# Tokens in order of their residue modulo four in the second attention layer of a 256-token decoder

## The chip, the cores and the metric

The kernel is one launch on one NeuronCore of a Trainium2 chip. The metric is the device time of that launch in microseconds (us), the median of several runs. TensorE (PE in the rows) multiplies matrices into PSUM, VectorE (DVE), ScalarE (ACT) and GpSimd (POOL) work element by element, and SyncE (SP) issues most of the DMAs. Every engine works through its own instructions in the order in which they are written; semaphores order the engines among each other.

## What is computed

The input is one sequence of 256 tokens of width 1024, in float32. Two decoder layers follow each other, each with a mixer and a SwiGLU. The first mixer (A) is stick-breaking attention with 16 heads of 64. The second (B) is an attention in three groups, each with its own queries, keys and values of 16 heads, whose outputs are mixed by their softmax denominators. Cut to what matters here:

```python
DILATED_GROUPS = ((128, 1), (512, 4), (2048, 16))      # (window, dilation)

def dilated_group_attention(qb, kk, vv, rel_bias, window, dilation):
    # queries and keys of one residue class modulo the dilation
    rel = Q_BLOCK + i - m
    band = (rel >= 0) & (rel <= window // dilation)
    bias = rel_bias[relative_bucket(rel * dilation)]
    s = einsum(qb, kk) * HEAD_DIM ** -0.5 + bias
    s = jnp.where(valid, s, NEG_INF)
    lse = logsumexp(s); p = exp(s - lse[..., None])
    return einsum(p, vv), lse

def mixer_b(xn, shared_kv, w_q, w_o, rel_bias):
    ...
    wts = jax.nn.softmax(lse, axis=0)                   # over the three groups
    o = jnp.sum(wts[..., None] * o, axis=0)
    return o.reshape(b, s, D_MODEL) @ w_o

# the layer around either mixer
x = x + rms_norm(h, g[1]);  h = swiglu(rms_norm(x, g[2]), w_gate_up, w_down);  x = x + rms_norm(h, g[3])
```

The mixing over the groups makes one softmax over the keys of all three groups together. In group 0 a token sees the 128 tokens before it and itself. In groups 1 and 2 it sees only tokens whose distance is a multiple of 4 or of 16, so only tokens of its own residue modulo 4.

## The kernel before, in words

Everything is written out by hand for each engine; there is no scheduler. Tokens stand in two tiles of 128 partitions (t = 0 and 1), tokens 0 to 127 and 128 to 255.

**Weights.** They come in 138 units of up to 1 MB. SP loads a unit into one of three raw buffers (L274 to L283; it waits for `lo_made`, which frees the buffer), ScalarE copies it as the high part `w_hi` (`hi`, L430), VectorE subtracts that and writes the low part `w_lo` (`lo`, L690), and TensorE multiplies high by high, high by low and low by high in float32r (`by_x`, L1091, and `by_w`, L1097). Six cut units can stand at a time.

**Stages.** Layer A: eight pairs of heads, each projected (`project_a`) while the pair before it is attended; each pair's output is turned into `ot`, high and low part (`cut_ot`, L770). Then the output projection (`out_proj`), the update of the residual `xn`, the SwiGLU. Layer B is the same with `step_b`: while the queries, keys and values of pair p are projected, the attention of pair p - 1 is worked on between these products. A step, in TensorE's order (L1381): `scores_b`, four blocks of columns, the nine transposes of head 0, a block, the nine transposes of head 1, a block, half the values, `outputs_b`, the other half.

**Attention B before the change.** For each head and group, `scores_b` (L1334) multiplies the first query tile by 128 keys (`short`) and the second by all 256 (`long`), in plain float32. VectorE adds the bias and takes the peak (`scored`, L882), 384 and 768 columns a head; ScalarE takes the exponential (L523), VectorE divides (`normalize`, L907), TensorE transposes 9 blocks of 128x128 into banks 4 to 6 of PSUM, the same three for both heads (L1366), so that the transposes of head 1 wait (L1363) until ScalarE has copied those of head 0 (`transposed_b`, L527). `outputs_b` (L1369) multiplies the transposed weights by the values: in each group 256 query columns for the first key tile, 128 for the second.

**The bias.** One line per head of 384 values is made at the start and stored in device memory (L390). In layer B, GpSimd loads for each head a band of 128x256 from it with one DMA (`head_bias`, L401 to L412), each partition one element further along, and adds it to the mask of all three groups, 768 columns in one instruction. VectorE waits for the bias of both heads of a pair before the peaks (L893).

**The output.** SP stores four pieces of 128x512 (L342 to L346) as their updates are made.

Of the kernel before, what the change touches and what calls it, by code (L numbers as in the profile page):

```python
# [28 lines left out]
SEQ = 256  # L29
P = 128  # L30
NT = SEQ // P
KT = D // P
NH = 16
# [6 lines left out]
NG = len(GROUPS)  # L40
BUCKETS = 32
# [22 lines left out]
def shape_constants():  # L64
# [7 lines left out]
    dist = P + i[:, None] - np.arange(2 * P)[None, :]  # L72
    mask = np.zeros((P, NG, 2 * P), np.float32)
    for g, (window, dilation) in enumerate(GROUPS):
        seen = (dist >= 0) & (dist % dilation == 0) & (dist // dilation <= window // dilation)
        mask[:, g] = np.where(seen, 0.0, OUTSIDE)

    n = np.maximum(np.arange(3 * P) - (P - 1), 0)
# [8 lines left out]
def build(nc, x, norm_gains, w_qkv_a, w_o_a, g_kv, w_kv_b, w_q_b, w_o_b, rel_bias, w_gate_up, w_down,  # L87
# [7 lines left out]
    out_dram = out[0].rearrange("(t p) d -> t p d", p=P)  # L95
# [7 lines left out]
    bias_rows = nc.dram_tensor("bias_rows", [NH, 3 * P], F32, kind="Internal").ap()  # L103

    with ExitStack() as ctx:
# [8 lines left out]
        bands = bass.AP(bias_rows.tensor, bias_rows.offset, [[3 * P, NH], [1, P], [1, 2 * P]])  # L114
# [12 lines left out]
        mask_b = sb("mask_b", [P, NG, 2 * P], BF16)  # L127
# [15 lines left out]
        select_in = carve(3 * P)  # L143
        rel_in = carve(NH)
        mask_in = carve(NG * 2 * P).rearrange("p (g s) -> p g s", g=NG)
        bias_out = carve(3 * P)
# [25 lines left out]
        W0, W1 = NG * P, NG * 2 * P  # L172
        prob = [carve(W0 + W1) for _ in range(2)]
        turned = [v.rearrange("p (g n) -> p g n", g=NG) for v in prob]
        bias = carve(2 * W1).rearrange("p (b g s) -> p b g s", b=2, g=NG)
        band = carve(2 * P)
# [25 lines left out]
        w_used = sem("w_used")  # L202
        x_in = [sem(f"x_in{t}") for t in range(NT)]
# [51 lines left out]

        def hidden_at(i):

            return slice(2, 4) if i == STEPS - 1 else slice(0, 2)


# [12 lines left out]
        def _(sp):  # L273
# [58 lines left out]
            sp.dma_start(mask_in, mask).then_inc(mask_in_s, 16)  # L332
            for u in range(4):
# [8 lines left out]
            for t in range(NT):  # L342
                for half in range(2):
                    sp.wait_ge(x_made, 6 * NT + 2 * t + half + 1)
                    cols = slice(HALF * half, HALF * half + HALF)
                    sp.dma_start(out_dram[t][:, cols], xn[:, t, cols]).then_inc(out_stored, 16)  # L346
            sp.wait_ge(out_stored, 32 * NT)
# [3 lines left out]
        def _(pool):  # L351
# [38 lines left out]
            pool.dma_start(bias_rows, bias_out[0:NH, :]).then_inc(bias_stored, 16)  # L390
            pool.wait_ge(bias_stored, 16)
# [9 lines left out]
            def head_bias(b, h):  # L401
# [4 lines left out]
                pool.dma_start(band, bands[ds(h, 1)].rearrange("h t s -> (h t) s")).then_inc(band_in, 16)  # L406
# [1108 lines left out]
```

## Time and profile before

| | |
|---|---|
| median of 3 runs | 793.88 us (793.18 to 794.0) |
| profiled execution | 794.14 us, span 792.5 us |
| TensorE busy | 782.9 us, 99% of the span |
| VectorE, ScalarE, GpSimd busy | 502.9, 378.2 and 61.7 us |
| granted clock of TensorE | full, 1.00 |
| DMA | 135.45 MB, mean 171 GB/s |

The matmul durations of the profile overlap, since the next product starts before the last has drained; what a matmul costs the path is read from the chain of work that ended last, which gives each only the time that it adds. Busy time of the other engines costs nothing while TensorE finds its inputs ready. A plain float32 matmul has two records in the trace, a transpose has one.

### The profile page before, as it was taken

The page shows a single profiled execution, that of the slowest core. Times are in us where ns is not written, and L with a number is a line of the kernel's source. Part 1 is how long each engine was busy: PE and PEld are TensorE (multiplying, and loading weights), DVE is VectorE, ACT ScalarE, POOL GpSimd, SP SyncE. Part 2 cuts the span into 40 slices and gives each one's busy share as a digit, 9 for nine tenths or more (in the row PEclk, how much of TensorE's full clock was granted, in tenths as well). Part 3 has the DMA queues.
Part 4 walks back from the last instruction along what each step waited for, and adds up shares of the span by engine and source line. Part 5 has one row for each costly group of instructions (what it writes and reads, how often), then busy time and mean ns, then how long its engine had stood idle before and what let it go on. Part 6 is the DMA issues. An engine that isn't in the chain of part 4 may idle for free.

```text
span 792.5 us, 12896 instructions
## 1 busy us (share of the span) xinstructions
PE 782.9 (99%) x4789; PEld 687.8 (87%) x4789; DVE 502.9 (63%) x632; ACT 378.2 (48%) x452; POOL 61.7 (8%) x76
## 2 busy tenths in 40 slices
PE   8999999999999999999999999999999999999997
PEld 7999978888888888998999999999988888888885
DVE  6888987764555646875746647567547755455453
ACT  5665667443434334934545435445357443443331
POOL 2000001100000000330201202112002000000000
PEclk9999999999999999999999999999999999999999
DMA  7534755676556555567556465474722874555601
GB/s 225 164 114 129 241 184 179 229 252 217 178 161 206 166 186 153 136 183 197 138 156 176 122 174 163 126 205 117 258 77 69 293 258 159 181 189 189 219 16 53
DMA packets 158818, 135.45 MB, mean 171 GB/s; under 512 B 5193, under 2 KB 149185, under 8 KB 158785
## 3 DMA queue, kind: packets, MB, share of 16 engines
q1 hardware_dynamic: 157312, 130.75, 52.7%
q0 software_dynamic: 1376, 4.22, 2.5%
q8 instruction: 21, 0.34, 0.2%
q14 instruction: 13, 0.10, 0.1%
q10 hardware_dynamic: 96, 0.04, 0.0%
HBM read 133.91 MB, written 1.07 MB: 170 GB/s over the span
## 4 chain that ended last, share of the span: by engine, by line
PE 94%; DVE 2%; ACT 1%; DMA 1%; issue 1%; SPq 0%; DVEq 0%; POOLq 0%; POOL 0%; ACTq 0%
PE ps L1093 20%; PE ps L1095 19%; PE ps L1094 19%; PE ps L1099 8%; PE ps L1101 8%; PE ps L1100 8%; PE ps L1376 2%; PE ps L1366 2%; PE ps L1241 1%; PE ps L1345 1%; DVE w_lo L693 1%; PE ps L1170 1%; PE ps L1339 1%; DMA raw<-in_w_q_b 1%; PE ps L1181 1%; PE ps L1148 1%
## 5 line engine op out<-in xcount | busy, mean ns | idle before, releaser
L693 DVE TENSOR_TENSOR w_lo<-raw,w_hi 128x2048 fp32r<-128x2048 f32 (+2 forms) x144 | 277.3, 1945 | 34.0 <-ACT w_hi L434 32.3
L434 ACT ACTIVATE w_hi<-raw 128x2048 fp32r<-128x2048 f32 (+2 forms) x144 | 232.3, 1637 | 45.3 <-DMA raw<-in_w_kv_b 11.4
L1093 PE MATMUL ps<-w_hi,xt 128*128 128x512 f32 x352 | 139.5, 396 | 0.0
L1095 PE MATMUL ps<-w_hi,xt 128*128 128x512 f32 x352 | 137.3, 390 | 0.0
L1094 PE MATMUL ps<-w_lo,xt 128*128 128x512 f32 x352 | 137.1, 389 | 0.0
L575 ACT ACTIVATE work<-ps,stat 128x256 f32<-128x256 f32 x44 | 20.9, 476 | 199.1 <-PE ps L1095 199.1
L1099 PE MATMUL ps<-xt,w_hi 128*128 128x256 f32 x384 | 110.2, 287 | 0.7 <-DVE w_lo L994 0.7
L1100 PE MATMUL ps<-xt,w_hi 128*128 128x256 f32 x384 | 108.6, 283 | 0.0
L1101 PE MATMUL ps<-xt,w_lo 128*128 128x256 f32 x384 | 108.6, 283 | 0.0
L1093 PE MATMUL ps<-w_hi,ot 128*128 128x512 f32 x240 | 94.9, 395 | 0.4 <-DVE w_lo L693 0.4
L1094 PE MATMUL ps<-w_lo,ot 128*128 128x512 f32 x240 | 93.5, 390 | 0.0
L1095 PE MATMUL ps<-w_hi,ot 128*128 128x512 f32 x240 | 93.5, 390 | 0.0
L1095 PEld LDWEIGHTS ps<-w_hi,xt 128*128 128x128 f32 x352 | 66.1, 188 | 14.0
L1093 PEld LDWEIGHTS ps<-w_hi,xt 128*128 128x128 f32 x352 | 66.1, 188 | 13.6 <-issue 0.6
L1094 PEld LDWEIGHTS ps<-w_lo,xt 128*128 128x128 f32 x352 | 66.2, 188 | 12.9
L1099 PEld LDWEIGHTS ps<-xt,w_hi 128*128 128x128 f32 x384 | 73.5, 191 | 4.3 <-issue 3.0
L1100 PEld LDWEIGHTS ps<-xt,w_hi 128*128 128x128 f32 x384 | 73.5, 192 | 0.0
L1101 PEld LDWEIGHTS ps<-xt,w_lo 128*128 128x128 f32 x384 | 73.5, 192 | 0.0
L953 DVE CAST ot<-ps 128x512 fp32r<-128x512 f32 x22 | 15.2, 692 | 78.2 <-PE ps L1241 78.2
L1099 PE MATMUL ps<-xkv,w_hi 128*128 128x256 f32 x192 | 55.5, 289 | 0.0
L1093 PEld LDWEIGHTS ps<-w_hi,ot 128*128 128x128 f32 x240 | 45.1, 188 | 10.8 <-DVE w_lo L693 1.0
L1101 PE MATMUL ps<-xkv,w_lo 128*128 128x256 f32 x192 | 54.3, 283 | 0.0
(130 smaller groups left out, 1100.9 us busy)
## 6 DMA issues: line engine op xcount, KB each, us to landing
raw<-in_w_gate_up SPq DMA_DIRECT2D x88, 512.0 KB, 4.7
raw<-in_w_kv_b SPq DMA_DIRECT2D x96, 256.0 KB, 3.6
raw<-in_w_down SPq DMA_DIRECT2D x22, 1024.0 KB, 4.9
raw<-in_w_q_b SPq DMA_DIRECT2D x48, 256.0 KB, 3.7
raw<-in_w_qkv_a SPq DMA_DIRECT2D x23, 512.0 KB, 4.8
raw<-in_w_o_a SPq DMA_DIRECT2D x4, 1024.0 KB, 5.4
raw<-in_w_o_b SPq DMA_DIRECT2D x4, 1024.0 KB, 5.2
work<-in_norm_gains POOLq DMA_DIRECT2D x4, 512.0 KB, 5.2
```

What stands on the lines that cost most here:

```text
L434: act.activation(w_hi[:, s % CUT, 0:size(s)], raw[:, s % RAW, 0:size(s)], ACT.Copy).then_inc(hi_made, 1)
L575: act.activation(silu[:, t, :], bank(4 + t, 0, FC), ACT.Silu, scale=x_rs(2 * l + 1, t)).then_inc(silu_made, 1)
L693: dve.tensor_tensor(w_lo[:, c, 0:n], raw[:, s % RAW, 0:n], w_hi[:, c, 0:n].bitcast(F32), ALU.subtract).then_inc(lo_made, 1)
L953: dve.tensor_copy(ot[:, 0, k, :], src).then_inc(ht_hi, 1)
L1093: mm(out, xs[0], ws[0], start=start, stop=False)
L1094: mm(out, xs[0], ws[1], start=False, stop=False)
L1095: return mm(out, xs[1], ws[0], start=False, stop=stop)
L1099: mm(out, ws[0], xs[0], start=start, stop=False)
L1100: mm(out, ws[0], xs[1], start=False, stop=False)
L1101: return mm(out, ws[1], xs[0], start=False, stop=stop)
L1366: inst = pe.transpose(bank(4 + g, P * n, P), prob[hh][:, at_:at_ + P], eye[:, :])
L1376: inst = mm(ps[DH * hh:DH * hh + DH, at_:512 * 7 + SEQ], vb[:, kt, P * g + DH * hh:P * g + DH * hh + DH], turned[hh][:, g, cols], start=g ...
```

## The change

From the first output projection on, the tokens stand in another order: all tokens with residue 0 modulo 4 first, then 1, 2 and 3, 64 each. Tile 0 holds residues 0 and 1, tile 1 residues 2 and 3. What it takes:

- The outputs of attention A are written to `ot` in the new order (VectorE reads PSUM with a step of four values).
- `x` is loaded a second time in the new order into `xn`, by four DMAs of 64x1024 from SP, behind the mask and before the weights of the output projection. The first update of `xn` waits for them.
- In groups 1 and 2 a tile only sees itself, so a query tile has 256 + 128 + 128 = 512 score columns in either tile, one bank of PSUM. The scores of the two heads stand in banks 2 to 5, the transposes of head 0 in banks 4 and 5 and of head 1 in banks 6 and 7; the wait of head 1's transposes for the copy of head 0's goes.
- The bias lines are seven per head, by difference of residues, and are stored with two DMAs. A head's band is 2x128x256 instead of 128x256, and comes with four DMAs of 64x4x64 (runs of 64 values, 256 bytes) instead of one of 128x256. The sum with the mask, still 768 columns, is in two instructions.
- The output is stored in eight pieces of 64x512, two of them from ScalarE's queue.

```diff
@@ sync
             sp.dma_start(mask_in, mask).then_inc(mask_in_s, 16)
+            sp.wait_ge(xt_done, 4)
+            sp.wait_ge(xsq_made, NT)
+            for r in range(R):
+                sp.dma_start(xn[RUN * (r % 2):RUN * (r % 2) + RUN, r // 2, :], by_residue(x[0])[r]).then_inc(x_again, 16)
...
-                    sp.dma_start(out_dram[t][:, cols], xn[:, t, cols]).then_inc(out_stored, 16)
+                    store(sp, t, half, 0)
+                    if t == 0:
+                        store(sp, t, half, 1)
@@ gpsimd
-            pool.dma_start(bias_rows, bias_out[0:NH, :]).then_inc(bias_stored, 16)
+            pool.dma_start(bias_rows[:, R - 1:2 * R - 1, 0:2 * RUN - 1], found[:, :, 1:2 * RUN]).then_inc(bias_stored, 16)
+            pool.dma_start(bias_rows[:, 0:R - 1, 0:2 * RUN - 1], found[:, 1:R, 0:2 * RUN - 1]).then_inc(bias_stored, 16)
...
-                pool.dma_start(band, bands[ds(h, 1)].rearrange("h t s -> (h t) s")).then_inc(band_in, 16)
-                pool.wait_ge(band_in, h * 16 + 16)
+                for r in range(R):
+                    pool.dma_start(band[RUN * (r % 2):RUN * (r % 2) + RUN, r // 2, :].rearrange("p (c n) -> p c n", c=R),
+                                   bands[r][ds(h, 1)].rearrange("h m c n -> (h m) c n")).then_inc(band_in, 16)
+                pool.wait_ge(band_in, (h * 16 + 16) * R)
...
-                pool.tensor_tensor(bias[:, b], mask_b[:, :, :],
-                                   band[:, ::-1].rearrange("p (g s) -> p g s", g=1).broadcast_to([P, NG, 2 * P]),
-                                   ALU.add).then_inc(bias_made, 1)
+                pool.tensor_tensor(ends[0], ends[1], turned_band, ALU.add)
+                pool.tensor_tensor(middle[0], middle[1], turned_band[:, 0:1, 0:P].broadcast_to([P, 2, P]), ALU.add
+                                   ).then_inc(bias_made, 1)
@@ scalar
-                act.activation(turned[hh], banks(4, NG, W0), ACT.Copy).then_inc(pt_made, 1)
+                act.activation(turned[hh], ps[:, 512 * (4 + 2 * hh):512 * (6 + 2 * hh)], ACT.Copy).then_inc(pt_made, 1)
...
+            for half in range(2):
+                act.wait_ge(x_made, 8 * NT - 1 + half)
+                store(act, NT - 1, half, 1)
@@ vector
+                    if b == 0 and t == 0 and half == 0:
+                        dve.wait_ge(x_again, 16 * R)
...
-                dve.tensor_copy(ot[:, 0, k, :], src).then_inc(ot_hi, 1)
+                hi_, lo_ = (ot[:, h, ds(k, 1), :].rearrange("p o (r m) -> p (o r) m", r=R) for h in range(2))
+                dve.tensor_copy(hi_, src).then_inc(ot_hi, 1)
                 dve.wait_ge(ot_hi, n)
-                dve.tensor_tensor(ot[:, 1, k, :], src, ot[:, 0, k, :].bitcast(F32), ALU.subtract).then_inc(ot_made, 1)
+                dve.tensor_tensor(lo_, src, hi_.bitcast(F32), ALU.subtract).then_inc(ot_made, 1)
...
+                cut_ot(j * 2 + a, bank(7, 0, SEQ).rearrange("p (m r) -> p r m", r=R), j * 2 + a + 1)
@@ tensor, scores_b
-                short(0)
-                long(0)
+                one(0, 0, 0, slice(0, SEQ))
+                one(1, 0, SEQ, slice(0, SEQ))
                 pe.wait_ge(qkb_made, j * 6 + 3 * a + 3)
-                short(1)
-                short(2).then_inc(s_done, 1)
-                long(1)
-                long(2).then_inc(s_done, 1)
+                one(0, 1, SEQ, slice(0, P))
+                one(0, 2, SEQ + P, slice(0, P)).then_inc(s_done, 1)
+                one(1, 1, 0, slice(P, SEQ))
+                one(1, 2, P, slice(P, SEQ)).then_inc(s_done, 1)
@@ tensor, transpose_b
-                if hh:
-                    pe.wait_ge(pt_made, h)
-                for g in range(NG):
-                    for n, at_ in enumerate((P * g, W0 + 2 * P * g, W0 + 2 * P * g + P)):
-                        inst = pe.transpose(bank(4 + g, P * n, P), prob[hh][:, at_:at_ + P], eye[:, :])
+                for t in range(NT):
+                    for n in range(4):
+                        kind = n if t == 0 else (n + 2) % 4
+                        inst = pe.transpose(bank(4 + 2 * hh + kind // 2, SEQ * (kind % 2) + P * t, P),
+                                            prob[hh][:, WB * t + P * n:WB * t + P * n + P], eye[:, :])
@@ tensor, outputs_b
-                    for kt, cols in ((0, slice(0, SEQ)), (1, slice(SEQ, SEQ + P))):
+                    for kt in range(NT):
+                        cols = slice(0, SEQ) if g == 0 else slice(P * kt, P * kt + P)
```

How TensorE's instructions stand in a step of layer B, before. This is inside the loop over the pairs; `work` holds queries, keys, weights and values of attention B, `xkv` the input of the projections. The three pieces are the scores, the transposes of head 0 and the outputs:

```order
1205 L1339 MATMUL ps<-work 128x128 x2
1206 L1345 MATMUL ps<-work 128x256 x2
1207 L1352 REGISTER_ALU
1208 L1339 MATMUL ps<-work 128x128 x4
1209 L1345 MATMUL ps<-work 128x256 x4
...
1312 L1366 MATMUL ps<-eye,work 128x128 x9
...
1389 L1095 MATMUL ps<-w_hi,xkv 128x384
1390 L1376 MATMUL ps<-work 64x256 x2
1391 L1376 MATMUL ps<-work 64x128 x2
1392 L1376 MATMUL ps<-work 64x256 x2
1393 L1376 MATMUL ps<-work 64x128 x2
1394 L1376 MATMUL ps<-work 64x256 x2
```

The same three pieces in the changed kernel:

```order
1205 L1363 MATMUL ps<-work 128x256 x4
1206 L1371 REGISTER_ALU
1207 L1363 MATMUL ps<-work 128x128 x8
...
1310 L1384 MATMUL ps<-eye,work 128x128 x8
...
1387 L1119 MATMUL ps<-w_hi,xkv 128x384
1388 L1396 MATMUL ps<-work 64x256 x4
1389 L1396 MATMUL ps<-work 64x128 x8
```

Scores and outputs stay at twelve matmuls each for a pair, with four wide ones where there were six; each head has eight transposes instead of nine. What stands around them has not moved.

GpSimd's queue at the start of attention B, before: the bias of the first two heads, then the start of the loop.

```order
33 L406 DMA work<-bias_rows 128x256 [waits x_made]
34 L410 TENSOR_TENSOR work<-mask_b,work 128x768 [waits band_in]
35 L406 DMA work<-bias_rows 128x256 [waits bias_made]
36 L410 TENSOR_TENSOR work<-mask_b,work 128x768 [waits band_in]
37 L416 UNCONDITIONAL_BRANCH
```

The same place in the changed kernel:

```order
34 L432 DMA work<-bias_rows 64x4x64 [waits x_made]
35 L432 DMA work<-bias_rows 64x4x64 x3
36 L440 TENSOR_TENSOR work<-mask_b,work 128x2x256 [waits band_in]
37 L441 TENSOR_TENSOR work<-mask_b,work 128x256
38 L432 DMA work<-bias_rows 64x4x64 [waits bias_made]
39 L432 DMA work<-bias_rows 64x4x64 x3
```

Each head now has four DMAs and two sums where it had one and one, in the same place of the queue.

## Rows read from the trace of the kernel before

**Rows 1.** The page: busy time, and the chain that ended last by engine.
```profile
PE 782.9 (99%) x4789; PEld 687.8 (87%) x4789; DVE 502.9 (63%) x632; ACT 378.2 (48%) x452; POOL 61.7 (8%) x76
...
PE 94%; DVE 2%; ACT 1%; DMA 1%; issue 1%; SPq 0%; DVEq 0%; POOLq 0%; POOL 0%; ACTq 0%
```

**Rows 2.** Waits of TensorE over the whole span: total us, times, longest.
```profile
PE ps L1404 <- DVE rows L983: 1.3, 1, 1.3
PE ps L1366 <- ACT work L530: 1.3, 1, 1.3
```

**Rows 3.** The chain, one later step of B: start us, us that it adds.
```profile
403.72 2.10 PE ps L1376 x24
...
410.19 0.42 PE ps L1339 x4
410.61 0.43 PE ps L1345 x4
411.05 0.44 PE ps L1339 x8
411.49 0.87 PE ps L1345 x8
...
424.06 0.98 PE ps L1366 x9
```

**Rows 4.** TensorE's transposes of B as a group: busy us, mean ns, idle before.
```profile
L1366 PE MATMUL ps<-eye,work 128*128 128x128 f32 x144 | 18.4, 273 | 1.3 <-ACT work L530 1.3
```

**Rows 5.** TensorE in the first step of B: start us, us, idle before.
```profile
357.99 1.15 PE L1366 MATMUL ps<-eye,work 128*128 128x128 f32 x9
...
363.30 1.17 PE L1366 MATMUL ps<-eye,work 128*128 128x128 f32 x9 [1.30 <-ACT work L530]
```

**Rows 6.** GpSimd from the first band on, the same columns.
```profile
326.34 0.62 POOL L406 DMA_DIRECT2D work<-bias_rows  x1
331.55 1.67 POOL L410 TENSOR_TENSOR work<-mask_b,work 128x768 f32<-128x768 bf16 x1 [4.58 <-DMA work<-bias_rows]
333.51 0.57 POOL L406 DMA_DIRECT2D work<-bias_rows  x1 [0.30 <-POOL work L410]
336.75 1.65 POOL L410 TENSOR_TENSOR work<-mask_b,work 128x768 f32<-128x768 bf16 x1 [2.67 <-DMA work<-bias_rows]
...
354.17 1.66 POOL L410 TENSOR_TENSOR work<-mask_b,work 128x768 f32<-128x768 bf16 x1 [2.97 <-DMA work<-bias_rows]
...
381.50 1.66 POOL L410 TENSOR_TENSOR work<-mask_b,work 128x768 f32<-128x768 bf16 x1 [24.46 <-DVE stat L885]
```

**Rows 7.** VectorE in the first step of B.
```profile
344.65 1.75 DVE L693 TENSOR_TENSOR w_lo<-raw,w_hi 128x1536 fp32r<-128x1536 f32 x1
346.32 0.55 DVE L885 CUSTOM_DVE_ANT_1 work<-ps,work 128x384 f32<-128x384 f32 x1
...
354.13 2.44 DVE L915 TENSOR_SCALAR work<-work,stat 128x384 f32<-128x384 f32 x2
```

**Rows 8.** DMA issues: count, KB of each, median us to landing.
```profile
raw<-in_w_q_b SPq DMA_DIRECT2D x48, 256.0 KB, 3.7
...
work<-in_norm_gains POOLq DMA_DIRECT2D x4, 512.0 KB, 5.2
work<-bias_rows POOLq DMA_DIRECT2D x16, 128.0 KB, 3.5
...
out_x<-xn SPq DMA_DIRECT2D x4, 256.0 KB, 2.1
```

**Rows 9.** SP's queue between the layer A loads: start us, us.
```profile
82.78 1.32 SPq L332 DMA_DIRECT2D work<-in_mask  x1
90.53 0.38 SPq L282 DMA_DIRECT2D raw<-in_w_o_a  x1
```

**Rows 10.** VectorE at the last cut of layer A.
```profile
119.36 0.42 DVE L772 CAST ot<-ps 128x256 fp32r<-128x256 f32 x1 [1.50 <-PE ps L1183]
119.82 0.42 DVE L774 TENSOR_TENSOR ot<-ps,ot 128x256 fp32r<-128x256 f32 x1
```

More of the change, by code:

```diff
@@ L40 @@
 NG = len(GROUPS)
+R = GROUPS[1][1]
+RUN = SEQ // R
 BUCKETS = 32
@@ L70, in shape_constants @@
     square = np.stack([eye, later, strict, np.ones((P, P), np.float32)], 1)
-    dist = P + i[:, None] - np.arange(2 * P)[None, :]
-    mask = np.zeros((P, NG, 2 * P), np.float32)
-    for g, (window, dilation) in enumerate(GROUPS):
+    token = R * (np.arange(SEQ) % RUN) + np.arange(SEQ) // RUN
+    parts = []
+    for t, g, keys in ((0, 0, SEQ), (0, 1, P), (0, 2, P), (1, 0, SEQ)):
+        window, dilation = GROUPS[g]
+        dist = token[P * t:P * t + P, None] - token[None, 0:keys]
         seen = (dist >= 0) & (dist % dilation == 0) & (dist // dilation <= window // dilation)
-        mask[:, g] = np.where(seen, 0.0, OUTSIDE)
-    n = np.maximum(np.arange(3 * P) - (P - 1), 0)
+        parts.append(np.where(seen, 0.0, OUTSIDE))
+    mask = np.concatenate(parts, 1).astype(np.float32)
+    n = np.maximum((R * (np.arange(2 * RUN)[None, :] - RUN) + np.arange(R)[:, None]).reshape(-1), 0)
     exact = BUCKETS // 2
@@ L110, in sem @@
             return ctx.enter_context(nc.semaphore(name))
-        bands = bass.AP(bias_rows.tensor, bias_rows.offset, [[3 * P, NH], [1, P], [1, 2 * P]])
+        bands = [bass.AP(bias_rows.tensor, bias_rows.offset + 2 * RUN * r,
+                         [[(2 * R - 1) * 2 * RUN, NH], [1, RUN], [2 * RUN, R], [1, RUN]]) for r in range(R)]
         raw = sb("raw", [P, RAW, UNIT])
@@ L171, in build @@
         vb = carve(NT * NG * P).rearrange("p (t n) -> p t n", t=NT)
[L172 to L176, printed above, removed]
+        WB = 4 * P
+        prob = [carve(NT * WB) for _ in range(2)]
+        turned = prob
+        bias = carve(2 * (WB + SEQ)).rearrange("p (b s) -> p b s", b=2)
+        band = carve(NT * SEQ).rearrange("p (t s) -> p t s", t=NT)
         def column(first):
@@ L202, in build @@
         w_used = sem("w_used")
+        x_again = sem("x_again")
         x_in = [sem(f"x_in{t}") for t in range(NT)]
@@ L254, in arrived, with store, by_residue @@
             return 16 * sum(parts(u) for u in range(s % RAW, s + 1, RAW))
+        def store(queue, t, half, r):
+            cols = slice(HALF * half, HALF * half + HALF)
+            queue.dma_start(by_residue(out[0])[2 * t + r][:, cols], xn[RUN * r:RUN * r + RUN, t, cols]
+                            ).then_inc(out_stored, 16)
         def hidden_at(i):
             return slice(2, 4) if i == STEPS - 1 else slice(0, 2)
+        def by_residue(v):
+            return v.rearrange("(m r) d -> r m d", r=R)
         def x_block(k, t, tiles=1):
@@ L1335, in scores_b, with one @@
                 heads = [slice(DH * hh, DH * hh + DH) for hh in range(2)]
-                def short(g):
+                def one(t, g, at_, keys):
                     for hh, r in enumerate(heads):
-                        inst = mm(bank(2 + 3 * hh, P * g, P), qb[r, g, 0:P], kb[r, g, 0:P], start=True, stop=True)
-                    return inst
-                def long(g):
-                    for hh, r in enumerate(heads):
-                        at_ = 512 * (3 + 3 * hh) + SEQ * g
-                        inst = mm(ps[:, at_:at_ + SEQ], qb[r, g, P:SEQ], kb[r, g, :], start=True, stop=True)
+                        inst = mm(bank(2 + 2 * hh + t, at_, keys.stop - keys.start), qb[r, g, P * t:P * t + P],
+                                  kb[r, g, keys], start=True, stop=True, skip_group_check=True)
                     return inst
```

62 lines of the change are left out of this document (26 added, 36 removed).

## The prediction

> **What bounds the kernel now.** I read the page first: TensorE is busy for 99% of the span and 94% of the chain that ended last is its work [rows 1]. Then its waits: over the whole span it waited 1.3 us before its first instruction, 1.3 us once for a copy of ScalarE, and the other entries of the list are under a microsecond each [rows 2]. So this kernel is a string of matmuls, and a change moves its time in two ways only: by the columns that TensorE has to stream, and by an input that comes late enough to make it wait. The chain says what a matmul adds to the string. Its records there, unlike the busy times, don't overlap [rows 3]. After that I looked at who feeds layer B beside the weights: GpSimd with the bias. In later steps its sum is ready and idles 24.46 us for the buffer that VectorE frees; only in the first step is it close [rows 6, 7].
>
> **What TensorE saves, step by step.** A plain float32 matmul has two records. In the scores, 8 records of 256 columns take 0.87 us and 8 of 128 columns 0.44 us [rows 3], so a matmul of 256 columns costs 0.217 us and one of 128 costs 0.11 us.
>
> - Scores: before, 6 matmuls of 256 and 6 of 128 a pair, 6 x 0.217 + 6 x 0.11 = 1.96 us (the chain has 0.42 + 0.43 + 0.44 + 0.87 = 2.16, of which 0.2 is the start of the group, which stays). After, 4 of 256 and 8 of 128: 1.75. Saved 0.21.
> - Outputs: the same counts before and after. Before they add 2.10 us [rows 3], 1.96 and the start. Saved 0.21.
> - Transposes: 9 add 0.98 us [rows 3], 0.109 each. Two fewer a pair: saved 0.22.
>
> That is 0.64 us a pair, and with 8 pairs (the 144 transposes of the trace are 8 x 18 [rows 4]) 5.2 us.
>
> The rate of the outputs could be another after the change, where eight matmuls of 128 columns stand in a row, which before came two at a time. In the scores four of them already stand in a row, and go at the rate of their columns (the 0.44 us for 8 records). So I take no loss; it is a rival below.
>
> On the price of float32 the Trainium skill has another number: "True FP32: 4 passes through PE array" (FP8 and Floating Point Precision, section TensorE Precision Notes). The trace shows two records for such a matmul, and the 0.217 us for 256 columns. By the page's four passes at the full clock, 256 columns would take an estimated 0.43 us, the savings of scores and outputs would double, and the sum would come out 3.4 us lower than mine. The measured duration decides here.
>
> **The wait that goes.** In the first step of B the transposes of head 1 start at 363.30 us after 1.30 us of idle time, for ScalarE's copy of head 0 out of the banks that both heads share [rows 5]. After the change each head has its own banks, so this wait has no object. What is late next at this place is `norm_made` of head 1, whose two multiplications ended with those of head 0 well before (354.13 + 2.44 = 356.57 for head 0, about 1.2 us more for head 1 [rows 7]), 4 us ahead. The copies of both heads are needed by the outputs some 8 us later. I take the full 1.3 us. In no other step did TensorE wait there, since the idle time of the group is this one wait [rows 4].
>
> **What is added.**
>
> - The bias lines: one matmul of 512 columns instead of 384, 0.11 us more on the path, at the start of the kernel. The second store of the lines has 200 us of cover until the first band.
> - `x` again: 1 MB in four DMAs on SP's queue. What stands behind them are the weights of the output projection. SP's last issue before was at 82.78 us and took 1.32, the next was at 90.53, when its buffer came free [rows 9]. Four issues of 0.4 to 1.3 us end by 89.4 at the latest. So SP is ready in time, and its queue holds nothing else meanwhile. The user, the first update of `xn`, comes after the last cut of layer A, which stood at 119.82 [rows 10], 30 us later. Cost 0; with the cover gone, one landing, about 4 us (a 256 KB load lands in 3.7 [rows 8]).
> - The step of four in VectorE's read of PSUM for `ot`: two instructions of 0.42 us for each pair [rows 10]. No row shows a strided read from PSUM. Lower end 0 (the count of elements is the same), upper end twice the time, 0.9 us a pair. VectorE is busy for 63% of the span, so only the last pair, on which the output projection waits, can put it on the path: 0 to 0.9 us, and I take 0.
> - Less work for VectorE and ScalarE in B (1024 instead of 1152 columns a head in peaks, exponential, division and copy): off the path, 0.
> - The stores: the last one was 256 KB and landed in 2.1 us [rows 8]. Now two of 128 KB go from two queues at the same time. Bounds -0.5 to +0.6 us; I take 0.
>
> **The bands are the open cost.** Four DMAs of 256 runs instead of one of 128 rows, twice the bytes, for each of 16 heads. Call D the time from the first issue of a head to the last landing. Before, D was 5.2 us for head 0 (326.34 to 331.55) and 3.2 for head 1 [rows 6]. Bias of both heads was ready at 336.75 + 1.65 = 338.4, and VectorE asked for it at 346.32, behind a cut of weights [rows 7]. With two heads one after the other, the bias is ready at 326.3 + 2D + 2 x 1.8 (the sums, a little more in two parts) + 0.6 between = 330.5 + 2D. It is on time up to D = 7.9. Queued behind the waiting VectorE are the peaks, two cuts of weights and the division; the transposes of head 0, at 357.99, had 1.4 us of room behind the division's end at 356.57, and that division took 2.44 us because a GpSimd sum ran from 354.17 to 355.83, which will now come later. With shorter peaks that gives some 2 us of room, so TensorE begins to wait at about D = 9.
>
> For D I have: one issue of 128 rows takes 0.57 us and lands in 3.5 (median) [rows 6, 8]. Lower end: four issues at 0.57, the last landing 3.5 to 5.2 after its own, D = 5.2 to 6.9. If an issue goes with its runs (256 instead of 128), it takes 1.1 us and D is 7 to 8.6. Upper end: everything goes with the runs, 1024 instead of 128, and D is 8 x 3.5 = 28. Against this end speaks that SP's loads of 256 KB, in 512 runs of 512 bytes, land in 3.7 us, as quickly as a band of 128 runs of 1 KB in 3.5, and that a load of four times a band's bytes on GpSimd's own queue needs 5.2 [rows 8]. I take D = 7, near the issue rows: ready at 344.5, no wait. In later steps a band of D = 7 stands against 24 us of idle time: 0.
>
> There the skill warns of a trap (SBUF — State Buffer, section SBUF: two separate sides): while VectorE runs an instruction in its two-port mode, GpSimd can't write the descriptors of its DMAs. By it a band that meets such an instruction is longer by that instruction. No row here separates this from the landing times of 3.2 and 5.2 us that they had anyway; it would push D up, to the side of the second rival.
>
> **The sum.** 794.14 (profiled execution: span 792.5 and 1.6 around it) - 5.2 - 1.3 + 0.1 = 787.7 us. The profiled execution stands 0.3 us over the median of 793.88, so 787.5 against the median; I say 787.7.
>
> **Rivals.**
>
> 1. The removed wait is replaced. In the first step the copy was late because ScalarE stood behind weights that had just landed; TensorE, now 1.3 us early, could wait for the same weights a little later. For it: this is the only step in which anything fed TensorE late. Against: the wait list shows no other wait in B. 787.7 + 1.3 = 789.0 us.
> 2. The first bias comes late, D between 9 and 12: TensorE waits 2 x (D - 9), at D = 10.5 3 us. For it: four issues in a row of a shape that no row has. 790.7 us.
> 3. The slower side, the same place with pieces that count: from D = 12.2 the stall of 2 x (12.2 - 9) = 6.4 us eats all that was saved, and at D = 14 it is 10 us, 797.7. Above D = 14 two bands and two sums (2 x 14 + 3.6) no longer fit in a step of 32 us and every pair waits. Against it speak the 512-run loads at 3.7 us.
> 4. Short matmuls in a row are bound by something else than columns. If each of the outputs' eight short matmuls cost what a wide one does, they would add 8 x 0.107 = 0.86 us a pair to the forecast, 6.9 us, and it would be 794.6, no change. The scores' row speaks against it.
> 5. The page's four passes: 784.3. The two records speak against it.
>
> **Chances.** Forecast 0.68, rival 1 0.10, rival 2 0.12, rival 3 0.06, rival 4 0.02, rival 5 0.02. A difference of 0.2% (1.6 us) is what a measurement of this kernel can tell. Faster than 792.3 are the forecast, rivals 1 and 5 and nearly all of rival 2: 0.91. Slower is rival 3, 0.06; rival 4 and the edge of rival 2 lie between, 0.03. The range reaches down by the store's 0.5 us and a little of the rates, 786.5, and up through rivals 1 and 2 at their middle, 791.0.
>
> **What would show it.** In the chain of the changed kernel a pair's scores add 1.95 us (2.16 before), 8 transposes 0.87, the outputs 1.9, and a step of the loop is 0.64 us shorter. TensorE's list of waits has no entry for ScalarE's copy. GpSimd's last sum of head 1 ends before 346.3 us, and VectorE has no wait for it. If instead VectorE's first peak starts late behind GpSimd and TensorE waits at its first transposes, it is rival 2 or 3, and the last landing of a head gives D. If TensorE's time in the loop fell by less than 0.6 us a step with no waits, the prices by columns were wrong.

## The result, and the profile after

| | before | after |
|---|---|---|
| median | 793.87 us (793.18 to 794.0) | 787.89 us (787.68 to 788.29) |
| profiled execution, span | 794.14, 792.5 us | 787.89, 786.2 us |
| TensorE busy | 782.9 us | 777.0 us |
| DMA | 135.45 MB | 138.65 MB |

The ratio is 0.9927 (95% interval 0.991 to 0.9944): 6.0 us faster, at 787.9 where 787.7 was forecast. In every comparison below the kernel before was run again on the same chip, and each ratio is against that run. The kernel after was repeated beside the first group of experiments alone (after_again); where a later one is said to be over it, two chips are compared, on which the kernel before took 793.2 to 793.7 us.

The page of the kernel after, busy times and then the chain by engine, which answer to [rows 1]:

```profile
PE 777.0 (99%) x4773; PEld 684.9 (87%) x4773; DVE 497.7 (63%) x632; ACT 374.8 (48%) x452; POOL 104.5 (13%) x141
...
PE 97%; DVE 2%; ACT 1%; issue 0%; DVEq 0%; POOLq 0%; POOL 0%; ACTq 0%
```

TensorE still fills the span, with less to do. GpSimd is busy for 104.5 us instead of 61.7. TensorE's list of waits (total us, times, longest), which answers to [rows 2]:

```profile
PE ps L1425 <- DVE rows L1007: 1.3, 1, 1.3
PE ps L1123 <- DVE w_lo L1018: 0.7, 2, 0.5
```

The wait for ScalarE's copy is gone and nothing stands in its place. The chain through one later step of the loop (start us, us that it adds), which answers to [rows 3]:

```profile
400.69 1.89 PE ps L1396 x24
...
406.95 1.96 PE ps L1363 x24
...
420.61 0.87 PE ps L1384 x8
...
432.27 1.89 PE ps L1396 x24
```

Outputs (L1396) 1.89 instead of 2.10, scores (L1363) 1.96 instead of 2.16, transposes (L1384) 0.87 instead of 0.98 for each head. From outputs to outputs a step takes 432.27 - 400.69 = 31.58 us. In the kernel before the outputs are at 403.72 [rows 3], and in the next step at

```profile
435.94 2.10 PE ps L1376 x24
```

so a step took 32.22 us there. That is 0.64 less. The first step on TensorE, with idle time in brackets, answers to [rows 5]:

```profile
357.28 1.04 PE L1384 MATMUL ps<-eye,work 128*128 128x128 f32 x8
361.03 1.04 PE L1384 MATMUL ps<-eye,work 128*128 128x128 f32 x8
```

Head 1's transposes follow head 0's after 3.75 us instead of 5.31, and no bracket stands behind them. GpSimd at the first bands, which answers to [rows 6]:

```profile
325.87 2.54 POOL L432 DMA_DIRECT2D work<-bias_rows  x4
333.18 1.17 POOL L440 TENSOR_TENSOR work<-mask_b,work 128x512 f32<-128x512 bf16 x1 [4.77 <-DMA work<-bias_rows]
334.31 2.19 POOL L441 TENSOR_TENSOR work<-mask_b,work 128x256 f32<-128x256 bf16 x1
336.80 2.45 POOL L432 DMA_DIRECT2D work<-bias_rows  x4 [0.30 <-POOL work L441]
342.93 1.18 POOL L440 TENSOR_TENSOR work<-mask_b,work 128x512 f32<-128x512 bf16 x1 [3.67 <-DMA work<-bias_rows]
344.05 0.68 POOL L441 TENSOR_TENSOR work<-mask_b,work 128x256 f32<-128x256 bf16 x1
...
379.08 1.18 POOL L440 TENSOR_TENSOR work<-mask_b,work 128x512 f32<-128x512 bf16 x1 [11.66 <-DVE stat L911]
```

From the first issue to the last landing D is 333.18 - 325.87 = 7.3 us for head 0 and 6.1 for head 1; 7 was taken. The bias is ready at 344.05 + 0.68 = 344.73, forecast 344.5. VectorE asks for it at 346.28, 1.6 us later (below), and has no wait. In the next step the bias still idles 11.66 us for its buffer, where it was 24.46 (and 17.17 in the step behind that, where it was 22.95). The same stretch on VectorE, which answers to [rows 7], with the one before it:

```profile
333.39 2.57 DVE L726 TENSOR_TENSOR w_lo<-raw,w_hi 128x1536 fp32r<-128x1536 f32 x1
338.75 1.75 DVE L726 TENSOR_TENSOR w_lo<-raw,w_hi 128x1536 fp32r<-128x1536 f32 x1
344.17 2.18 DVE L726 TENSOR_TENSOR w_lo<-raw,w_hi 128x1536 fp32r<-128x1536 f32 x1
346.28 0.68 DVE L911 CUSTOM_DVE_ANT_0 work<-ps,work 128x512 f32<-128x512 f32 x1
```

The DMA issues of the changed transfers (count, KB of each, median us to landing), which answer to [rows 8]:

```profile
work<-bias_rows POOLq DMA_DIRECT2D x64, 64.0 KB, 4.2
...
xn<-in_x SPq DMA_DIRECT2D x4, 256.0 KB, 6.7
out_x<-xn SPq DMA_DIRECT2D x6, 128.0 KB, 2.4
...
out_x<-xn ACTq DMA_DIRECT2D x2, 128.0 KB, 2.9
```

SP at the second load of `x`, which answers to [rows 9]:

```profile
83.02 2.75 SPq L354 DMA_DIRECT2D xn<-in_x  x4
90.06 0.39 SPq L300 DMA_DIRECT2D raw<-in_w_o_a  x1
```

The four issues are over at 85.8, and the weights behind them go out at 90.06 as their buffer comes free. The load itself landed in 6.7 us, where 3.7 had been taken; with 30 us of cover that is of no account. The read of PSUM in steps of four, which answers to [rows 10]:

```profile
118.89 0.42 DVE L808 CAST ot<-ps 128x256 fp32r<-128x256 f32 x1 [1.51 <-PE ps L1207]
```

It costs what the read in a row cost: 0.42. Last, the end of the kernel: VectorE's last update of the residual and the stores of the kernel after,

```profile
778.67 4.62 SPq L267 DMA_DIRECT2D out_x<-xn  x6
781.39 1.41 DVE L777 SCALAR_TENSOR_TENSOR xn<-work,stat,xn 128x512 f32<-128x512 f32 x2 [0.29 <-POOL stat L382]
782.17 1.38 ACTq L267 DMA_DIRECT2D out_x<-xn  x2
```

and of the kernel before:

```profile
785.84 4.49 SPq L346 DMA_DIRECT2D out_x<-xn  x4
...
788.55 1.41 DVE L742 SCALAR_TENSOR_TENSOR xn<-work,stat,xn 128x512 f32<-128x512 f32 x2 [0.29 <-POOL stat L359]
```

The last update ends at 782.80 of 786.2 after and at 789.96 of 792.5 before: 3.4 us of stores instead of 2.5. So the end gives back 0.9 us. Up to the last update the kernel is 788.55 - 781.39 = 7.16 us ahead, of which 0.63 is a start that varies from run to run: the first matmul of the weights is at 9.64 here and at 10.27 before, behind the same five and four matmuls on `rows`, and in the other runs below anywhere from 9.19 to 10.46, in kernels with the change and without. In the two spans, 792.5 and 786.2, this start and the loss at the end all but cancel.

### The profile page after: what moved, and what is told of

Read it like the earlier page. It is cut to its first block, busy times and chain, and to the rows that moved or that the text cites. A ratio compares the mean times of both kernels' runs of the same rounds, so it can differ in the third digit from the quotient of the medians.

```text
span 786.2 us, 13014 instructions
## 1 busy us (share of the span) xinstructions
PE 777.0 (99%) x4773; PEld 684.9 (87%) x4773; DVE 497.7 (63%) x632; ACT 374.8 (48%) x452; POOL 104.5 (13%) x141
## 2 busy tenths in 40 slices
DMA packets 160514, 138.65 MB, mean 176 GB/s; under 512 B 6105, under 2 KB 150081, under 8 KB 160481
## 4 chain that ended last, share of the span: by engine, by line
PE 97%; DVE 2%; ACT 1%; issue 0%; DVEq 0%; POOLq 0%; POOL 0%; ACTq 0%
PE ps L1117 20%; PE ps L1119 20%; PE ps L1118 19%; PE ps L1123 9%; PE ps L1125 9%; PE ps L1124 9%; PE ps L1363 2%; PE ps L1396 2%; PE ps L1384 2%; PE ps L1265 1%; PE ps L1194 1%; PE ps L1205 1%; PE ps L1172 1%; PE ps L1138 1%; DVE w_lo L726 1%; PE ps L1425 1%
## 5 line engine op out<-in xcount | busy, mean ns | idle before, releaser
L726 DVE TENSOR_TENSOR w_lo<-raw,w_hi 128x2048 fp32r<-128x2048 f32 (+2 forms) x144 | 284.8, 1996 | 33.6 <-ACT w_hi L464 31.9
L379 POOL TENSOR_SCALAR stat<-stat 128x1 f32<-128x1 f32 x16 | 10.7, 669 | 388.0 <-ACT work L480 366.1
```

The lines of the kernel that those rows point to most:

```text
L726: dve.tensor_tensor(w_lo[:, c, 0:n], raw[:, s % RAW, 0:n], w_hi[:, c, 0:n].bitcast(F32), ALU.subtract).then_inc(lo_made, 1)
```

## Experiments

They are variants of the kernel after, unless said otherwise, and each puts one term back or enlarges one.

### The terms of the sum

**after_again**: the kernel after, unchanged, as the yardstick for the three runs that follow.

> The changed kernel itself, once more, as the reference for the runs beside it. Both theories: 787.9 us within 0.4, 5.9 to 6.1 us under the kernel before.

788.36 us (787.77 to 788.59), ratio 0.993 (0.9918 to 0.9942) to the kernel before, here 793.69.

**wait_back**: TensorE waits before head 1's transposes for ScalarE's copy of head 0 again.

```
                 for hh in range(2):
+                    if hh:
+                        pe.wait_ge(pt_made, h)
```

> The changed kernel with the wait of head 1's transposes for ScalarE's copy of head 0 put back; nothing else. Theory (the wait is worth its idle time, in the first step only): TensorE waits there once, for 0.9 to 1.5 us, and the kernel takes 789.1 us, 1.2 us over the changed one; from the second step on no wait. Rival (whatever TensorE gains there it waits again a little later, for weights of the first step): the same 787.9 us. A third possibility, that the wait costs something in each step by the way TensorE is released: 8 x 0.1 more, over 789.8.

789.56 us (788.65 to 789.8), 1.2 us over after_again. In the profile one entry came back to TensorE's list, 1.1 us, once. It stands in the first step:

```profile
362.61 1.06 PE L1386 MATMUL ps<-eye,work 128*128 128x128 f32 x8 [1.09 <-ACT work L560]
```

The term of 1.3 us is right, in place and, by the medians of six runs, in size. What one profile shows of it is less firm, because the copy waits for weights that have just landed: in the kernel after it ended 0.7 us after head 1's transposes had begun (361.75 against 361.03), in after_again 0.3 us, and a wait there would have been about as long as that.

**cols_back**: the columns that the change took out are streamed again (128 columns of scores, one transpose and 128 columns of outputs a head), with the new order of tokens and all else kept.

```
+                one(1, 2, P, slice(P, SEQ))
...
+                inst = pe.transpose(bank(4 + 2 * hh, SEQ + P, P), prob[hh][:, WB + 3 * P:WB + 3 * P + P], eye[:, :])
...
+                for hh in range(2):
+                    mm(bank(7, 0, P)[DH * hh:DH * hh + DH, :], vb[:, 0, DH * hh:DH * hh + DH],
+                       turned[hh][:, 0:P], start=True, stop=False, skip_group_check=True)
```

> The changed kernel with the columns of before put back as repeats: for each head one more score matmul of 128 columns, one more output matmul of 128 columns and one more transpose, all of them writing what they or the next one write anyway. Theory (columns and transposes are the price, 0.64 us a pair): 8 x 0.65 = 5.2 us over the changed kernel, 793.1 us, and a step of the loop is 32.2 us again. Rival (part of the saving came from the order of wide and narrow matmuls or from the banks, not from the columns): clearly under 5 us, 791 or less.

793.73 us (793.21 to 794.77), 5.4 us over after_again and level with the kernel before (ratio 1.0001, 0.9993 to 1.001). Its chain:

```profile
401.77 0.37 PE ps L1394 x4
402.14 1.74 PE ps L1401 x24
408.26 2.18 PE ps L1363 x28
...
434.03 0.37 PE ps L1394 x4
```

Scores are back at 2.18, outputs at 0.37 + 1.74 = 2.11, a step at 434.03 - 401.77 = 32.26 us. So the columns are worth 5.4 us, all that the loop had saved, and nothing that can be measured is left for the order in which the new kernel reads its operands. That the time is level with the kernel before is two terms against each other: ScalarE's copy is still not waited for, 1.2 us less, and the stores still cost 0.9 us more (below).

**no_x_again**: no second load of `x`, so that the residual stands in the old order of tokens under updates in the new one; the work is the same.

```
-                sp.dma_start(xn[RUN * (r % 2):..., r // 2, :], by_residue(x[0])[r]).then_inc(x_again, 16)
...
-                    if b == 0 and t == 0 and half == 0:
-                        dve.wait_ge(x_again, 16 * R)
```

> The changed kernel without the second load of x, so that the residual stands in the old order of tokens under updates in the new one; the work is the same. Theory (the load is hidden on SP's queue and in the DMA engines): 787.9 us, within 0.3 of the changed kernel. Rival (it holds back the weights of the output projection, or the first update): 0.5 to 4 us faster than the changed kernel.

788.06 us (787.41 to 788.73), 0.3 us under after_again, and the two runs' ranges overlap: the second load of 1 MB costs nothing that can be measured.

### The stores at the end

**tail_sp**: all eight stores from SP's queue, none from ScalarE's.

```
-                    if t == 0:
-                        store(sp, t, half, 1)
+                    store(sp, t, half, 1)
```

> The changed kernel with all eight stores of 64x512 on SP's queue. Theory (ScalarE's queue is slow to issue and land): 0.3 us less than the changed kernel, 787.6, since SP needs 0.5 us for the issue of one more store but each lands in 2.4 instead of 2.9 us. Rival (two queues at once are a help): 0.4 us more, 788.3.

789.15 us (788.75 to 789.32), ratio 0.9945 to its kernel before (793.21). Its last update starts at 782.05 and ends 3.9 us before the span of 787.4, where the kernel after has 3.4. By the tail alone it is 0.5 us slower, by the medians 1.0 (bands_8, which loses nothing, has 788.15 on the same chip). The rival was right: the second queue helps, but doesn't bring the 2.5 us of before back.

**tail_whole**: four stores as before, each with both residues, so that the side in memory has an outer dimension of two.

```
+                    cols = slice(HALF * half, HALF * half + HALF)
+                    sp.dma_start(by_residue(out[0])[2 * t:2 * t + 2][:, :, cols], xn[:, t, cols]
+                                 ).then_inc(out_stored, 16)
```

> The changed kernel with four stores of 128x512 from SP as before the change, each of them two residues; none from ScalarE. In the trace of the changed kernel the end of the span comes 3.4 us after the last update's end, before the change 2.5 us. Theory (ScalarE's queue and the two stores issued at once cost it): the end comes 2.5 us after the update again and the kernel takes 787.0 us, 0.9 less than the changed one. Rival (rows that lie 16 KB apart in device memory cost it, or chance): 787.9 us.

804.58 us (804.16 to 805.06), 16 us slower than the kernel after: the expectation missed by far. A window of its end (start and end, length, then busy us of TensorE's matmuls, its weight loads, VectorE, ScalarE and GpSimd with their instructions, granted clock, share of the 16 DMA engines, GB/s), which the windows up to 800 repeat:

```profile
784.00:788.00 4.00, 0.00 (x0) 0.00 (x0) 0.00 (x0) 0.00 (x0) 0.00 (x0) 0.50 0.13 51
```

The last update ended at 783.1, and then nothing but the stores runs for 19.7 us, at 0.13 of sixteen engines: two. The kernel after, in the same place:

```profile
780.00:784.00 4.00, 0.00 (x0) 0.00 (x0) 2.10 (x3) 0.31 (x2) 0.86 (x2) 0.96 0.70 161
784.00:786.20 2.20, 0.00 (x0) 0.00 (x0) 0.00 (x0) 0.00 (x0) 0.00 (x0) 0.50 0.47 170
```

So the split into one store for each residue, which the change makes, is what keeps the DMA engines at work. The Trainium skill has the rule (DMA: Bandwidth & Descriptors, section "Why a DMA increments its semaphore by 16 and not by 1"): a DMA is spread over the largest number of engines up to 16 that divides the outermost dimension of both sides. With an outer dimension of 2 these would be two engines of sixteen, and the trace's 0.13 agrees.

**split_old**: the kernel before, with its stores cut into two of 64 rows and the last two on ScalarE's queue, as the change does; the rows in memory stay contiguous.

```
+        def store(queue, t, half, r):
+            cols = slice(HALF * half, HALF * half + HALF)
+            queue.dma_start(out_dram[t][64 * r:64 * r + 64, cols], xn[64 * r:64 * r + 64, t, cols]
+                            ).then_inc(out_stored, 16)
```

> The kernel before the change with only its stores in the changed form: eight of 64x512, two of them from ScalarE's queue, rows next to each other in device memory. Theory (the 0.9 us that the changed kernel's end is longer by come from smaller pieces on two queues): the end of the span comes 3.4 us after the last update and the kernel takes 0.9 us more than before. Rival (they come from rows 16 KB apart): as before, 2.5 us after the last update.

794.5 us (793.64 to 796.09), 1.0 us over the kernel before, here 793.49 (ratio 1.0014, 1.0003 to 1.0024). Its update ends at 788.62 of 792.0, so the stores take 3.4 us again. They land in 2.4 us on SP's queue and 2.8 on ScalarE's, the figures of the kernel after (2.4 and 2.9) without its order of rows. So the 0.9 us belong to the smaller pieces on two queues, not to the rows four apart.

### How late a band may come

**bands_8**: eight DMAs of 32 partitions a head instead of four of 64, the same bytes and runs.

```
+                    for m in range(2):
+                        at_ = RUN * (r % 2) + 32 * m
+                        pool.dma_start(band[at_:at_ + 32, r // 2, :]..., bands[r][ds(h, 1)]...[32 * m:32 * m + 32]
```

> The changed kernel with eight DMAs of 32x4x64 for each band instead of four of 64x4x64; same bytes and same runs. It tells what an issue costs and where the cover ends. Theory 1 (an issue costs per DMA, 0.6 us): eight take 4.9 us, a band D = 9.7 for head 0 and 8.6 for head 1, the first bias is ready at about 348.5 us, VectorE waits 2 us for it, and TensorE little or nothing: 787.9 to 788.5. Theory 2 (an issue costs per run): the same 2.5 us for eight, D = 7, no wait of VectorE, 787.9.

788.15 us (787.89 to 788.72), ratio 0.9933, no loss. GpSimd, then VectorE:

```profile
326.70 4.44 POOL L434 DMA_DIRECT2D work<-bias_rows  x8
336.00 1.18 POOL L443 TENSOR_TENSOR work<-mask_b,work 128x512 f32<-128x512 bf16 x1 [4.86 <-DMA work<-bias_rows]
```

```profile
348.47 0.69 DVE L914 CUSTOM_DVE_ANT_0 work<-ps,work 128x512 f32<-128x512 f32 x1 [1.72 <-issue]
```

Half the runs in each DMA, and an issue still takes 4.44 / 8 = 0.56 us, after 2.54 / 4 = 0.64 in the kernel after. So an issue goes by the DMA and not by its runs. D is 9.3 and 7.8 us, VectorE waits 1.72 us, and TensorE not at all.

**bands_16**: sixteen DMAs of 16 partitions, for every head, by the same edit with `range(4)` and 16.

> The changed kernel with sixteen DMAs of 16x4x64 for each band. Theory 1 (0.6 us per issue): D = 14.6 for head 0 and 13.5 for head 1, the first bias ready at about 358 us, 12 us behind VectorE's question at 346.3. By the prediction's threshold (TensorE waits once the bias is over 2 us late) the first step loses 9 to 10 us: 797.5 us, and the later steps nothing or little, since two bands and their sums are 31.7 us in a step of 31.6. Theory 2 (per run): 787.9, no wait. A third: the later steps lose too, since two bands no longer fit, over 805.

797.38 us (797.03 to 797.97), ratio 1.005 (1.0037 to 1.0064). The time is the expected one, and its reason is another. In the first step D is 10.1 (326.08 to 336.16), VectorE waits 4.06 us, and TensorE 0.25; the expected time was met by chance. The loss stands at the end of the layer:

```profile
PE ps L1141 <- DVE xn L780: 5.1, 2, 4.9
...
PE ps L1387 <- DVE work L942: 0.9, 2, 0.6
```

GpSimd issues the gains of the following norm too, and VectorE needs them:

```profile
589.29 0.58 POOL L399 DMA_DIRECT2D work<-in_norm_gains  x1 [16.79 <-issue]
```

```profile
595.88 1.29 DVE L769 TENSOR_TENSOR work<-ps,work 128x512 f32<-128x512 f32 x2 [6.87 <-DMA work<-in_norm_gains]
```

In the kernel after the issue comes 0.3 us after the last outputs have ended, here 3.4 us after them. VectorE then waits 6.87 us for the landing, and TensorE 4.93 us for VectorE, from 592.95 to 597.88. From 597 to 603 the granted clock is 0.50, the lower of its two levels (1.2 of 2.4 GHz), and from 604 it is full again. The waits (4.9 + 0.9) and some 2.7 us lost to the half clock make 8.5 of the 9.2 us over bands_8; the rest has no row. GpSimd was late in every step (in the last one VectorE waits 8.24 us for it before its peaks), but its last sum had ended at 572.5, long before the outputs. So it was not a queue that ran behind which held the gains back; what did, no row shows, and it stays open.

**first_16** and **first_32**: to have the first step alone, only heads 0 and 1 get their bands in 16 and in 32 DMAs.

```
+                if isinstance(h, int) and h < 2:
+                    for r in range(R):
+                        for m in range(4):
+                            at_ = RUN * (r % 2) + 16 * m
```

> The changed kernel with sixteen DMAs of 16x4x64 for the bands of the first two heads only, four for all others. With sixteen for all heads VectorE waited 4 us in the first step and TensorE 0.3, and the 9.2 us of loss came at the end of layer B. Theory (first-step lateness of 4 us is covered, the loss there was GpSimd's queue running behind to the last step): 788.3 us, 0.3 over the changed kernel. Rival (the prediction's own threshold, 2 x (D - 9) with D = 10.1): 790.1 us.

790.0 us (788.63 to 790.83), ratio 0.9952 (0.9935 to 0.997). VectorE's first peak, and then TensorE's entry:

```profile
350.90 0.69 DVE L920 CUSTOM_DVE_ANT_0 work<-ps,work 128x512 f32<-128x512 f32 x1 [4.24 <-issue]
```

```profile
PE ps L1393 <- DVE work L948: 1.0, 1, 1.0
```

The median lies with the rival, the wait of 1.0 us between the two, and the runs spread over 2.2 us. By the time this is inconclusive. The trace says how much room there was: 4.24 us of wait on VectorE became 1.0 on TensorE, so the room behind VectorE is 3.2 us, where the prediction had "some 2". The 2 are there: in the kernel after, head 0's division ends at 355.32 and TensorE comes at 357.28. The rest is time that VectorE loses beside GpSimd's sums in the kernel after and does not lose here: the cut before the peaks takes 1.75 us instead of 2.18, and the division 1.43 instead of 2.27. In bands_16 it takes 0.88, the room is 3.8, and the same 4 us of lateness cost TensorE 0.25. So the room depends on what GpSimd runs meanwhile.

> The changed kernel with 32 DMAs of 8x4x64 for each of the first two bands, four for all others. An issue takes 0.51 to 0.6 us: D = 18.5, both biases ready at about 367 us, VectorE 20 us late. Theory (4 us of it are covered, the rest stops TensorE): 16 us over the changed kernel, 804 us, and a lower granted clock right after the stop. By the prediction's threshold (2 x (18.5 - 9)) 19 us, 807. If TensorE could go on with projections meanwhile, less than 12 us.

810.65 us (810.09 to 811.86), ratio 1.0216. More than either figure. VectorE, an entry of TensorE's list, and two windows of all engines:

```profile
370.13 0.69 DVE L920 CUSTOM_DVE_ANT_0 work<-ps,work 128x512 f32<-128x512 f32 x1 [23.68 <-issue]
```

```profile
PE ps L1132 <- DVE w_lo L735: 18.1, 1, 18.1
```

```profile
380.00:382.00 2.00, 2.00 (x11) 2.00 (x10) 2.00 (x4) 1.49 (x1) 1.29 (x3) 0.51 1.14 317
382.00:384.00 2.00, 2.00 (x19) 2.00 (x18) 1.41 (x1) 0.30 (x1) 0.00 (x0) 1.00 0.83 185
```

The wait isn't where the prediction had put it. TensorE stops at the products of the next weights (L1132), because VectorE's cut of these weights (L735) is queued behind the peaks. With 0.9 us before the transposes it waits 19.0 us. Of the 22.3 us over after_again 3.3 are left, and the clock accounts for them: TensorE went on at 374.59, and from there to 382 the granted clock was 0.50, so 6.5 us of matmuls and 0.9 of waiting passed at half speed, and half of the 6.5 is lost.

**both_back**: wait_back and cols_back in one kernel, so that the kernel after has the work of the kernel before again.

> The changed kernel with both put back: the repeats of columns and transposes, and the wait for ScalarE's copy. If the two are independent, 5.5 + 1.2 = 6.7 us over the changed kernel, 794.8 us, and so about 1 us over the kernel before; that one is what the change adds elsewhere (0.9 at the end, 0.1 for the bias matmul). If the wait is hidden once the columns are back, 793.6.

794.17 us (793.39 to 795.76), 0.7 us over the kernel before, 793.49 (ratio 1.0005, 0.9995 to 1.0015). Its entry for ScalarE's copy:

```profile
PE ps L1387 <- ACT work L560: 0.4, 1, 0.4
```

It is 0.4 us and not 1.1. TensorE came to head 0's transposes at 358.31 instead of 357.62, but 0.54 of that is the start of the run (first matmul of the weights at 10.36 instead of 9.82), and the columns account for about 0.2. Whether the columns hide a part of the wait is therefore not shown by this pair of profiles. What is left over the kernel before is of the size of the stores' 0.9 us, but the interval holds zero.

## Why the prediction was right, and where it was off

**The matmuls, 5.2 us: right in time, on a price that was misread.** A step of the loop is 0.64 us shorter, as forecast, and with the columns back the time rises by 5.4. The outputs add 1.89 us (1.9 forecast), so eight short matmuls in a row go by their columns, which refutes rival 4.

The 0.217 us for 256 columns is not what one matmul takes, though. Two rows of the kernel before, the first records of a step's scores and the four matmuls on `rows` near the start:

```profile
410.12 0.38 PE L1339 MATMUL ps<-work 64*128 64x128 f32 x2
```

```profile
8.14 1.89 PE L1404 MATMUL ps<-rows 128*128 128x256 f32 x8
```

The scores' records come in twos, one for each head, and in the trace the starts of two lie 0.006 us apart, while each lasts 0.27 to 0.38: the two heads' matmuls run at the same time. The heads' queries and keys stand on different halves of the 128 partitions. The outputs' records come in twos in the same way. A matmul without such a partner takes twice as long: eight records of 256 columns take 1.89 us on `rows`, 0.47 for each matmul, where they take 0.87 in the scores. The prediction divided the time of four matmuls, two at a time, by four. Its sum is right all the same, because every matmul that the change saves in the scores and outputs has its partner in the other head.

Where a matmul stands alone the price was too low. The one for the bias lines, before and after:

```profile
17.46 0.74 PE ps L1425 x2
```

```profile
16.82 0.96 PE ps L1446 x2
```

Its 128 more columns cost 0.22 us, where 0.11 was taken.

The prediction set the four passes of the Trainium skill (FP8 and Floating Point Precision, section TensorE Precision Notes) against its two records. The trace agrees with the page: the estimate of 0.43 us for 256 columns by its four passes is near the 0.47 measured on `rows`, and it is what two heads' matmuls take together in the scores (0.87 us for two such pairs). Rival 5 went wrong in doubling a saving that was already the time of both heads. It would have made 1.06 us a step; the trace has 0.64.

**The removed wait, 1.3 us: right.** With it back the time rises by 1.2, and the list shows 1.1. Rival 1 is refuted: nothing took its place.

**The bands at no cost: right, with the margin known now.** D was 7.3 and 6.1 where 7 was taken. The 6.1 lies in the prediction's lower end (5.2 to 6.9), the 7.3 in its middle case (7 to 8.6), in which an issue goes with its runs, but the reason of the lower end is the right one for both: an issue takes 0.64 us with 256 runs, hardly more than the 0.57 to 0.62 with 128 before [rows 6], and the last landing follows the end of the issues by 4.77 and 3.67 us. One reading was wrong without cost: the next sum of GpSimd was to come later than VectorE's division. It ran from 353.04 to 355.05, and the division beside it, from 353.05, took 2.27 us.

**The threshold of rivals 2 and 3: too early, and the end of it missed.** "TensorE begins to wait at about D = 9", with 2 x (D - 9). first_16 has D = 10.2 in the mean and waits 1.0 us, where this gives 2.3; bands_16 has 10.1 and waits 0.25 in its first step. With the same slope the waiting begins at D = 9.7 by the one and 9.9 by the other. For first_32 (D 21.3 and 18.6) the formula gives 22 us, and 19.0 were waited. The size of the stall is roughly as told, but past some point it is the cut of the next weights that TensorE waits for, and the half clock behind a long stop comes on top. That bands in more pieces for all heads cost at the end of the layer, not in its first step, was not among the rivals at all.

**The stores, taken at 0 with an upper bound of 0.6: the term that was off.** They cost 0.9 us in the pair of profiles and 1.0 in split_old, outside the bounds. The working had a gain in mind from half the bytes on two queues, but a piece of half the size doesn't land sooner: 2.4 us on SP's queue and 2.9 on ScalarE's, on which the last one goes, against 2.1 for the whole [rows 8].

**That the time was hit to 0.2 us is in part luck.** The terms as measured make -5.4 - 1.2 + 0.2 + 0.9 = -5.5 us, 0.9 less than the 6.4 of the sum. The measured differences are -5.3 (after_again) and -6.0 (the first comparison), so the first one happened to lie on the forecast's side. And the forecast started from a profiled execution that was 0.3 us over its median, while the profile of the kernel after began 0.6 us earlier than that of before.

**`x` again and the strided read: 0, right.** Without the load 0.3 us within the spread, and 0.42 us for the same read.

## What to carry to other kernels

Where TensorE is busy for 99% of the span, price a change by the records of the chain and look then for the one place in which an input is just in time; both main terms of this sum came out within 0.2 us. Before a price per matmul is carried to another place, look whether its records come in twos: a pair here took 0.22 us for 128 columns and a matmul alone took the same. Look at the outermost dimension of both sides of a DMA before you merge two into one: after the last update the stores took 19.7 us with a 2 there and 3.4 with a 64. What ends the kernel has no cover: count the last update's stores by issues and landings, not by bytes.

## What the runs showed that was not expected

- VectorE and GpSimd hold each other up. The cut of 128x1536, which normally takes 1.75 us (338.75 above), took 2.57 at 333.39, beside the sum of GpSimd that ran from 333.18; and GpSimd's sum of 256 columns took 2.19 us instead of 0.68, until 0.54 us after this cut had ended at 335.96. In bands_8 the band lands later, the same cut and the same sums don't meet, and they take 1.75, 1.18 and 0.68 us. At 344.17 the cut took 2.18 beside a sum of 256 columns that was already running and took its usual 0.68. All the cuts together went from 277.3 to 284.8 us; none of it reached TensorE.
- A DMA issued by GpSimd costs 0.51 to 0.64 us in all of these runs: 0.64 at 256 runs of 256 bytes, 0.56 at 128, 0.51 at 64 (8.19 us for 16), 0.54 at 32 (17.31 for 32).
- A stop of TensorE costs more than its own length. The granted clock was 0.50 after the stop of 4.9 us (bands_16) as after the one of 18.1 us (first_32), for 5 to 7 us of work each time: some 2.7 us beside 5.8 us of waits in the one, 3.3 beside 19.0 in the other. After the waits of 1.0 us or less it stayed full.
